# A kernel with three expert layers: when the last four ring weights of the two later layers are issued

## Chip, cores and metric

One core of a Trainium2 chip runs the whole program in one launch. The metric is device time in microseconds (us) of that core.

## What is computed

The reference is a model of three layers on 512 tokens of width 1024, in f32. The first layer has a mixer, a cross attention and a mixture of experts (32 experts of inner width 512). The two later layers have a token mixer and then a mixture of experts with 32 experts of inner width 256. Only the experts of the two later layers matter here:

```
grp_prob = softmax(xt @ w_rg + b_rg); the best group of 4, then the best 2 of its 8 experts
hid = silu(xe @ w_gate[e]) * (xe @ w_up[e]);  y = hid @ w_down[e]     # for each token of expert e
x = layernorm(alpha * x + weighted sum of the token's two y)
```

Each token goes to 2 of 32 experts, so the 1024 assignments make 32 tokens per expert on average.

## The kernel before

`moe` (line 785) is called three times: e0 for the first layer (its tiles begin with m_ or e_), e1 and e2 for the two later layers (r_, e_). It is one block with a program for each engine; order within an engine is program order, and engines meet only on semaphores.

**Routing.** VectorE (DVE) and TensorE (PE) choose experts and ranks and make a table of blocks: a block is up to 64 tokens (SLOTS) of one expert. In the two later layers all of this waits for the token mixer's result.

**Weights.** `ExpertRing` (line 735) is a ring of expert slots in SBUF. Each slot s has two parts, gate_up (part 0, 2048 KB in the later layers, loaded at L757) and down (part 1, 1024 KB, L760). The later layers have six slots, thus twelve parts in the order (0,0), (0,1), (1,0) to (5,1). The first four parts, "early", are issued during the token mixer. The other eight, "late", are issued at line 900 by SyncE (SP) at the start of `moe`, right behind the store of all token rows to DRAM (L899, 2048 KB). In e0 the ring has three slots, so six parts, of which three are early and three late. After the late loads SP waits for the table and then goes round `refill`: for expert e it waits until the expert's gate/up matmuls are done (gu_ready) and issues gate_up of expert e+6 into the slot, then waits for the expert's last output (y_ready) and issues its down part. All these loads are on one hardware DMA queue (q1).

**Tokens.** GpSimd (POOL) gathers the rows of each block from DRAM with an indirect DMA at L1246 into `landing[:, p]`, two buffers in turn, on the software queue (q0). `rows_gathered[p]` rises by 16 when such a gather has landed. The first two gathers wait for the stored rows and for `tokcol`, the token numbers made by DVE. DVE copies a landed block (L1156 for the first, L1159 for the second, L1178 for the others), PE turns it (L957, L959), DVE copies it to `xT` (L1151).

**Experts.** PE goes through the experts in order. For each it waits until gate_up has landed (line 979); each block has 32 matmul pairs for gate and up (L987, L989), a turn of the hidden rows (L967) and, once the down part has landed, eight matmuls (L1004). DVE copies the output (L1173), and POOL scatters it to DRAM (L1254). When all blocks are done, SP loads the outputs back (L924), and DVE adds and normalises.

```
def load_first(self, sp, parts):          # line 763
    for s, m in parts:
        self.load(sp, s, s, m)
...
pool.wait_ge(tokcol_ready, 1)             # line 1260
for n in range(2):
    gather(n, n)
```

Of the kernel before, what the change touches and what calls it, by code (L numbers as in the profile page):

```python
# [784 lines left out]
def moe(nc, name, k, x, rows_dram, h_rows, gain, ring, router, norm, alpha=1.0):  # L785
# [15 lines left out]
    with Stage(nc, name) as st:  # L801
# [57 lines left out]
        rows_gathered = [st.sem(f"rows_gathered{n}") for n in range(2)]  # L859
# [31 lines left out]
        def pairs_of_blocks(eng):  # L891

            return eng.value_load(pair_table[0:1, 0:1], min_val=1, max_val=MAX_BLOCKS // 2)

        with nc.Block() as block:
            @block.sync
            def _(sp):
                if h_rows is not None:
                    sp.dma_start(rows_dram.rearrange("(t p) d -> p t d", p=P), h_rows).then_inc(rows_stored, 16)  # L899
                ring.load_first(sp, ring.late)  # L900
                sp.wait_ge(table_ready, 2)

                def refill(turn_, s):

                    e = turn_ * RING + s
                    end = sp.value_load(table[0:1, 1, bass.ds(e, 1)], min_val=1, max_val=MAX_BLOCKS)
                    sp.wait_ge(gu_ready, end * 2)
                    ring.load(sp, e + RING, s, 0)
                    sp.wait_ge(y_ready, end)
                    ring.load(sp, e + RING, s, 1)  # L910

                with sp.Fori(0, TURNS - 1) as turn_:
                    for s in range(RING):
                        refill(turn_, s)
                for s in range(TAIL):
                    refill(TURNS - 1, s)

                n_pairs = pairs_of_blocks(sp)
                for n in range(2):
                    sp.wait_ge(y_stored[n], n_pairs * 16 + 32)  # L920
                for t in range(TT):
                    for j in range(2):
                        a = 2 * S * j + 2 * P * t
                        sp.dma_start(ring.back(j)[:, t, :], y_dram[a:a + 2 * P].rearrange("(p h) d -> p (h d)", p=P)  # L924
                                     ).then_inc(back_landed[j * TT + t], 16)
                    if norm.out is not None and t == 0:
                        for n in range(2):
                            sp.dma_start(norm_rows[:, n], norm.rows[n].partition_broadcast(P)).then_inc(norm_rows_landed, 16)
                if norm.out is not None:
                    for t in range(TT):  # L930
                        sp.wait_ge(finished, t + 1)
                        sp.dma_start(norm.out[t * P:(t + 1) * P], x[:, t, :]).then_inc(out_stored, 16)
                    sp.wait_ge(out_stored, 16 * TT)
# [1709 lines left out]
```

## Time and profile before

| | |
|---|---|
| time, median of 3 runs | 2899.93 us (2899.85 to 2900.85) |
| the profiled execution: its time, its span | 2899.57 us, 2896.9 us |
| PE, DVE, ACT, POOL busy | 84%, 45%, 32%, 13% |
| e1's block, from the store of rows to the last expert matmul | 1661.5 to about 1966 us |
| e2's block, the same | 2566.1 to about 2854 us |
| median time of a later gate_up load from issue to landing | 32.0 us |

"Span" is from the first to the last instruction on the core. In the windows view each row is a stretch of the span with each engine's busy time and number of instructions, the granted TensorE clock (1.00 is 2.4 GHz, 0.50 is 1.2 GHz), the mean busy share of the 16 DMA engines and the GB/s that they moved (a share can read a little over 1, since a packet counts to the stretch in which it starts). In the timeline a row is start, duration, engine, line, operation, operands, and in brackets the engine's idle time before it. "DMA to landing" is the time from an issuing instruction's start until the semaphore tells that the data has landed.

### The profile page before, as it was taken

Reading aid. Unit: us, or ns where it says so; the run is one execution under the profiler, and the core shown is the slowest. Engines: PE = TensorE matmul, PEld = TensorE weight load, DVE = VectorE, ACT = ScalarE, POOL = GpSimd, SP = SyncE. Lnnn points to the kernel's source line nnn. Section 1 sums busy time; section 2 is a strip of 40 time slices with the busy share of each in tenths; the row PEclk is TensorE's granted clock in tenths of the full one; section 3 lists DMA queues with packets and bytes.
Section 4 is the critical chain, followed back from the end, with each engine's and each line's share of the span. In section 5 each row is a group of like instructions: output and inputs, shape, how many; then the busy total and the mean of one; then the engine's idle time right before and its main releaser. Section 6 shows DMA issues by size and latency. Waiting matters only on the chain. (4 is left out here: it accounts for less than half of the span.)

```text
span 2896.9 us, 50154 instructions
## 1 busy us (share of the span) xinstructions
PE 2445.6 (84%) x18120; PEld 1919.4 (66%) x18121; DVE 1304.2 (45%) x2835; ACT 921.4 (32%) x1736; POOL 381.2 (13%) x710
## 2 busy tenths in 40 slices
PE   7987799698889868999898869995999989859783
PEld 6976698554445437776676857674777767857562
DVE  6465335421112125646553644335744844654334
ACT  3533333221111124235432323324334632223222
POOL 1000000121122110000000134430000000024332
PEclk9999899699999989999999879998999999969996
DMA  4201325599999953032122489994222222459994
GB/s 149 74 1 59 102 88 206 201 406 409 410 405 407 401 201 120 30 91 55 46 55 70 164 304 378 377 367 141 74 64 55 55 55 64 177 213 382 379 391 186
DMA packets 209397, 565.77 MB, mean 195 GB/s; under 512 B 26694, under 2 KB 170694, under 8 KB 184688
## 3 DMA queue, kind: packets, MB, share of 16 engines
q1 hardware_dynamic: 191200, 538.74, 50.0%
q0 software_dynamic: 18064, 25.23, 2.7%
q8 instruction: 86, 1.41, 0.2%
q14 instruction: 47, 0.39, 0.0%
HBM read 560.47 MB, written 36.18 MB: 206 GB/s over the span
## 5 line engine op out<-in xcount | busy, mean ns | idle before, releaser
L987 PEld LDWEIGHTS ps<-r_gate_up,e_xT 128*64 128x64 f32 x2272 | 263.8, 143 | 93.0 <-issue 89.3
L987 PE MATMUL ps<-m_gate_up,e_xT 128*64 128x256 f32 x1088 | 272.0, 414 | 62.1 <-DMA m_gate_up<-in_w_gate_up 61.3
L987 PE MATMUL ps<-r_gate_up,e_xT 128*64 128x128 f32 x2272 | 276.0, 282 | 43.9 <-DMA r_gate_up<-in_w_exp_gate_up 34.9
L1167 DVE TENSOR_TENSOR e_hid<-e_silu,ps 64x128 f32<-64x128 f32 (+1 forms) x210 | 70.2, 335 | 470.8 <-ACT e_silu L1029 467.4
L987 PEld LDWEIGHTS ps<-m_gate_up,e_xT 128*64 128x64 f32 x1088 | 160.9, 150 | 175.2 <-issue 112.1
L989 PE MATMUL ps<-r_gate_up,e_xT 128*64 128x128 f32 x2272 | 276.1, 282 | 0.0
L989 PE MATMUL ps<-m_gate_up,e_xT 128*64 128x256 f32 x1088 | 272.1, 414 | 0.0
L1029 ACT ACTIVATE e_silu<-ps 64x128 f32<-64x128 f32 (+1 forms) x210 | 63.8, 304 | 645.7 <-PE ps L989 645.7
L989 PEld LDWEIGHTS ps<-r_gate_up,e_xT 128*64 128x64 f32 x2272 | 263.7, 143 | 0.0
L2404 PE MATMUL ps<-t_hT,t0a_t0g_w 128*128 128x512 f32 x768 | 199.5, 411 | 4.6 <-DVE t0a_t0g_w L2426 2.4
L2404 PE MATMUL ps<-t_hT,t1a_t1g_w 128*128 128x512 f32 x768 | 199.1, 411 | 4.6 <-DVE t1a_t1g_w L2426 2.4
L1173 DVE TENSOR_SCALAR e_y<-ps 128x512 f32 x105 | 72.6, 691 | 249.1 <-PE ps L1004 225.4
L2404 PEld LDWEIGHTS ps<-t_hT,t0a_t0g_w 128*128 128x128 f32 x768 | 145.6, 194 | 45.9 <-issue 10.3
L2404 PEld LDWEIGHTS ps<-t_hT,t1a_t1g_w 128*128 128x128 f32 x768 | 145.3, 194 | 45.7 <-issue 10.3
L1029 ACT ACT_TABLE_LOAD x105 | 134.7, 1283 | 120.7 <-issue 119.9
L989 PEld LDWEIGHTS ps<-m_gate_up,e_xT 128*64 128x64 f32 x1088 | 160.8, 150 | 0.0
L1917 POOL TENSOR_TENSOR all_x<-all_x,t_merged 128x1024 f32<-128x1024 f32 x2 | 4.8, 2402 | 1142.0 <-PE ps L1750 1142.0
L1004 PE MATMUL ps<-r_down,e_hidT 128*64 128x512 f32 x568 | 137.5, 605 | 0.0
L1251 POOL COPY e_choicecur<-e_choicecol 128x1 uint32 x106 | 53.0, 500 | 586.0 <-DVE e_y L1173 586.0
L1246 POOL DMA_INDIRECT e_landing<-e_dram_rows,e_tokcur x115 | 116.6, 1014 | 59.4 <-issue 59.4
L1004 PE MATMUL ps<-m_down,e_hidT 128*64 128x512 f32 x544 | 124.2, 598 | 0.0
L1254 POOL DMA_INDIRECT e_dram_y<-e_y,e_choicecur x106 | 109.8, 1036 | 56.0 <-issue 55.8
(651 smaller groups left out, 4788.6 us busy)
## 6 DMA issues: line engine op xcount, KB each, us to landing
m_gate_up<-in_w_gate_up SPq DMA_DIRECT2D x32, 4096.0 KB, 38.4
r_gate_up<-in_w_exp_gate_up SPq DMA_DIRECT2D x64, 2048.0 KB, 32.0
m_down<-in_w_down SPq DMA_DIRECT2D x32, 2048.0 KB, 38.1
r_down<-in_w_exp_down SPq DMA_DIRECT2D x64, 1024.0 KB, 33.7
t0a_t0g_raw<-in_w_in SPq DMA_DIRECT2D x32, 512.0 KB, 3.8
t1a_t1g_raw<-in_w_in SPq DMA_DIRECT2D x32, 512.0 KB, 3.8
mixw_raw<-in_w_in SPq DMA_DIRECT2D x10, 1024.0 KB, 5.2
xaw_raw<-in_w_kv_x SPq DMA_DIRECT2D x8, 1024.0 KB, 5.3
```

What stands on the lines that cost most here:

```text
L987: nc.tensor.matmul(ps_gu[q][0:SLOTS], xT[:, c, :], ring.gu[s][:, 0, c, span], start=c == 0, stop=c == DC - 1)
L989: last = nc.tensor.matmul(ps_gu[q][SLOTS:P], xT[:, c, :], ring.gu[s][:, 1, c, span], start=c == 0, stop=c == DC - 1)
L1004: last = nc.tensor.matmul(ps_y[h * SLOTS:(h + 1) * SLOTS], hidT[:, f, :], ring.wd[s][:, f, h * 512:(h + 1) * 512], start=f == 0, stop=f == ...
L1029: nc.scalar.activation(silu[SLOTS:P, q], ps_gu[q][0:SLOTS], ACT.Silu).then_inc(silu_ready, 1)
L1167: vec.tensor_tensor(hid[SLOTS:P, q], silu[SLOTS:P, q], ps_gu[q][SLOTS:P], ALU.mult).then_inc(hid_ready, 1)
L1173: vec.tensor_scalar(y[:, bass.ds(g % 2, 1)].rearrange("p one d -> p (one d)"), ps_y, 1.0, None, ALU.mult).then_inc(y_copied, 1)
L1246: nc.gpsimd.indirect_dma_start(landing[:, p], None, rows_dram, bass.IndirectOffsetOnAxis(tokcur[p][:], 0), bounds_check=S - 1, oob_is_err= ...
L1251: nc.gpsimd.tensor_copy(choicecur[p][:], choicecol[:, bass.ds(n, 1)]).then_inc(choicecur_ready, 1)
L1254: nc.gpsimd.indirect_dma_start(y_dram, bass.IndirectOffsetOnAxis(choicecur[p][:], 0), y[:, p], None, bounds_check=4 * S - 1, oob_is_err=Fa ...
L1917: link(nc.gpsimd.tensor_tensor(x[:, t, :], x[:, t, :], finish[0][:, 0], ALU.mult))
L2404: last = nc.tensor.matmul(ps[:, 6, :], w[:, p, q, :], self.hT[:, r, q, :], start=q == 0 and p == r, stop=q == DC - 1 and p == LO)
```

## The change

In SP's program of `moe`, the late parts are issued in two portions. The first four late parts, (2,0) to (3,1), are issued as before. If there are more (there are in e1 and e2, not in e0), SP waits until both `rows_gathered` semaphores have reached 16, that is until the first two gathers have landed, and then issues (4,0), (4,1), (5,0), (5,1).

```
                 if h_rows is not None:
                     sp.dma_start(rows_dram.rearrange("(t p) d -> p t d", p=P), h_rows).then_inc(rows_stored, 16)
-                ring.load_first(sp, ring.late)
+                ring.load_first(sp, ring.late[:4])
+                if ring.late[4:]:
+                    for n in range(2):
+                        sp.wait_ge(rows_gathered[n], 16)
+                    ring.load_first(sp, ring.late[4:])
                 sp.wait_ge(table_ready, 2)
```

## Rows read from the trace of the kernel before

**Rows 1.** Waits of PE, 1690 to 1860 us (e1): total us, times, longest.
```profile
PE ps L957 <- DVE e_gathered L1156: 12.2, 1, 12.2
```

**Rows 2.** Waits of PE, 2690 to 2860 us (e2).
```profile
PE ps L987 <- DMA r_gate_up<-in_w_exp_gate_up: 25.4, 10, 3.7
```

**Rows 3.** Timeline of SP in e1: the first, third and fourth gate_up refill.
```profile
1707.58 0.35 SPq L757 DMA_DIRECT2D r_gate_up<-in_w_exp_gate_up  x1
...
1740.01 0.33 SPq L757 DMA_DIRECT2D r_gate_up<-in_w_exp_gate_up  x1
...
1746.49 0.33 SPq L757 DMA_DIRECT2D r_gate_up<-in_w_exp_gate_up  x1
```

**Rows 4.** Timeline of SP in e2: store of rows, part (3,1), first and fourth refill.
```profile
2566.08 0.38 SPq L899 DMA_DIRECT2D e_dram_rows<-all_x  x1
...
2570.11 1.29 SPq L760 DMA_DIRECT2D r_down<-in_w_exp_down  x1
...
2605.38 0.35 SPq L757 DMA_DIRECT2D r_gate_up<-in_w_exp_gate_up  x1
...
2624.90 0.33 SPq L757 DMA_DIRECT2D r_gate_up<-in_w_exp_gate_up  x1
```

**Rows 5.** Timeline of POOL: gathers of e0 (first), e1 (both), e2 (second).
```profile
553.02 1.14 POOL L1246 DMA_INDIRECT e_landing<-e_dram_rows,e_tokcur  x1 [0.65 <-issue]
...
1683.04 2.43 POOL L1246 DMA_INDIRECT e_landing<-e_dram_rows,e_tokcur  x1 [0.57 <-issue]
...
1686.47 0.96 POOL L1246 DMA_INDIRECT e_landing<-e_dram_rows,e_tokcur  x1 [0.54 <-issue]
...
2591.40 0.97 POOL L1246 DMA_INDIRECT e_landing<-e_dram_rows,e_tokcur  x1 [0.54 <-issue]
```

**Rows 6.** L1246 by source, e1's gathers issued at 1683.0, 1686.5, 1734.3: to landing.
```profile
DMA to landing us min/median/max: 9.2/9.2/9.2
...
DMA to landing us min/median/max: 8.1/8.1/8.1
...
DMA to landing us min/median/max: 3.0/3.0/3.0
```

**Rows 7.** The chain that ended last, in e2: start, us, what.
```profile
2587.97 8.25 DMA e_landing<-e_dram_rows,e_tokcur
```

**Rows 8.** L1246 by source, e0's first gather, then its second: issue to landing.
```profile
DMA to landing us min/median/max: 3.7/3.7/3.7
...
DMA to landing us min/median/max: 3.1/3.1/3.1
```

**Rows 9.** Windows around e0's first gathers (553) and in e1.
```profile
553.00:559.00 6.00, 1.35 (x9) 1.25 (x9) 0.69 (x1) 0.00 (x0) 5.25 (x10) 0.50 0.20 59
...
1699.00:1700.00 1.00, 1.00 (x22) 1.00 (x20) 0.29 (x1) 0.27 (x1) 0.00 (x0) 0.92 1.13 336
1702.00:1708.00 6.00, 6.00 (x84) 4.69 (x83) 2.36 (x5) 2.25 (x5) 2.19 (x5) 1.00 0.05 16
1732.00:1740.00 8.00, 8.00 (x115) 6.42 (x111) 2.88 (x6) 2.38 (x6) 4.33 (x8) 1.00 0.14 48
1740.00:1940.00 200.00, 187.64 (x2393) 144.93 (x2391) 74.49 (x142) 63.26 (x142) 88.86 (x171) 0.98 1.01 390
```

**Rows 10.** Windows in e2.
```profile
2566.00:2588.00 22.00, 5.58 (x48) 5.28 (x48) 15.76 (x74) 2.79 (x3) 0.39 (x3) 0.50 0.97 384
2604.00:2608.00 4.00, 4.00 (x45) 2.59 (x43) 0.98 (x2) 1.24 (x4) 0.00 (x0) 1.00 0.93 243
2608.00:2840.00 232.00, 204.08 (x2556) 156.77 (x2554) 79.81 (x150) 67.55 (x151) 93.28 (x180) 0.97 1.00 381
```

**Rows 11.** In e2, (3,1) at L760, then the first refill at L757: issue to landing.
```profile
DMA to landing us min/median/max: 19.9/19.9/19.9
...
DMA to landing us min/median/max: 8.8/8.8/8.8
```

**Rows 12.** The page's DMA issues, later layers' gate_up: KB each, median us to landing.
```profile
r_gate_up<-in_w_exp_gate_up SPq DMA_DIRECT2D x64, 2048.0 KB, 32.0
```

## The prediction, on record before the result

> **What bounds the kernel now.** I read the page first (PE busy 84%, DMA near its top in the expert stages), then the waits of PE in e1 and e2, then SP's and POOL's timelines at the start of both layers, and last the windows, which show what the DMA engines do.
>
> At the start of each later expert layer PE stands idle until the first gathered block has been copied: 12.2 us in e1 [rows 1]. The last part of that wait is the gather itself. It takes 9.2 us in e1 [rows 6] and 8.25 us in e2, where it lies on the chain that ended last [rows 7]. In e0, where the DMA engines are at share 0.20 [rows 9], the same instruction's gathers land after 3.7 and 3.1 us [rows 8]. So about 5 us of each first gather looks like company on the DMA engines: the eight late parts.
>
> Then the layers differ. In e1 the DMA engines run dry twice, share 0.05 at 1702 to 1708 and 0.14 at 1732 to 1740, while PE is busy all the time [rows 9]: PE sets the pace, since SP issues a refill only when PE has used a slot up. From 1740 to 1940 the share is 1.01. In e2 the engines never run dry: 0.93 at the worst spot, then 1.00 from 2608 to 2840 [rows 10], and in the later part PE waits ten times for gate_up [rows 2]. From its first load on, e2 is a queue of loads whose sum sets the end. That is the reader's main picture: the same edit comes to a stage with DMA slack and to one without.
>
> **The change, part by part.** The store of rows and the first four late parts are issued as before. Behind them SP now waits for two gathers. Queued behind the waiting instruction are the last four late parts (two of 2048 KB [rows 12], two of half that: 6.29 MB) and then every refill. PE waits for these in the end. POOL's gathers wait for nothing that stands behind SP's wait, only for the store ahead of it.
>
> *The first gather.* Rows and first four parts are 2.10 + 6.29 = 8.39 MB. In e2 the engines move 384 GB/s x 22.0 us = 8.45 MB by 2588.0 [rows 10], and part (3,1) lands at 2570.11 + 19.9 = 2590.0 [rows 4, 11]: 2 us after the bytes are counted, as the engines don't end together. The first gather's instruction takes 2.43 us in e1 and e2 [rows 5] (DVE scales x beside it; this stays), so its packets meet nearly empty engines once the last four parts are held back. In e0 the gather landed 3.7 - 1.14 = 2.56 us after its instruction ended [rows 5, 8]. With that:
> - e1: 1683.04 + 2.43 + 2.56 = 1688.0 in place of 1692.2, gain 4.2 us.
> - e2: 2587.97 + 2.43 + 2.56 = 2593.0 in place of 2596.2, gain 3.3 us.
> Bounds: none of it (the gather stays as long), and 4.6 and 3.7 us if the 3.1 us row is the measure (3.1 - 0.97 = 2.1 us after the end). I take the first row, as it is the same instruction in the same place.
>
> The Trainium skill ("DMA: Bandwidth & Descriptors", section "Queues, rings and completion order") says that each DMA engine takes turns between the queue rows that have work, a packet at a time. The gather's queue would then never wait for the weights' backlog, and holding weights back would free little; 9.2 against 3.7 us speaks for more than such sharing, but the page gives a rival, worked out below from rows.
>
> *e1.* PE starts 4.2 us earlier. It starts at 1.2 GHz, and the clock goes to 2.4 GHz just after 1699 [rows 9], some 7 us after the gather's landing; if the rise follows the earlier start a little less closely, some tenths are lost: I count 4.0. Are the held parts in time? SP goes on at 1686.47 + 3.1 = 1689.6 [rows 5, 8]; with 0.7 us until bytes flow (0.97 of 22 us in [rows 10]), 6.29 MB at 385 GB/s (16.3 us) and the 2 us of uneven ends, (5,1) lands at 1708.6. PE uses slot 4 after the fourth refill is issued, at 1746.49 - 4 = 1742 [rows 3]: over 30 us of cover. Refill one would be issued at 1703.4 and be done about 1717, refill two about 1728, and the third is issued at 1740.01 - 4.2 = 1735.8 [rows 3]: the engines still run dry before it, with some 7 us to spare. From the third refill on everything is as before, 4 us earlier. What is late next is DMA, but it moves with it. e1: -4.0 us, between -4.6 and 0.
>
> *e2.* The gain of 3.3 us at PE's start is worth nothing, since loads set the end. What counts is when the queue has moved the same bytes. Before, the first refill's gate_up landed at 2605.38 + 8.8 = 2614.2 [rows 4, 11]. After: SP goes on at 2591.40 + 3.1 = 2594.5 [rows 5, 8], bytes flow from 2595.2. Ahead of that landing are 6.29 + 2.10 MB of weights: 8.39 / 0.385 = 21.8 us, and 2 us of uneven ends: 2619.0. That is 4.8 us later; with the third and fourth gathers among them I take 5.0. Afterwards the share is 1.00 up to 2840, so nothing gives it back. Counted in idle time instead, the engines stand from 2588.0 to 2595.2, less 0.2 for two small gathers, against 0.07 x 4 = 0.3 us before [rows 10]: 6.7 us, the upper end. If the rate is 5% better with less company, 3.5 us, the lower end. The held parts are in time: (5,1) at 2595.2 + 16.3 + 2 = 2613.5, slot 4 wanted after 2624.90 - 3.3 = 2621.6 [rows 4].
>
> *e0.* Its late list has three parts; nothing changes.
>
> **Sum.** -4.0 + 5.0 = +1.0 us on the profiled execution's 2899.57 us (span 2896.9 and 2.7 around it) is 2900.6; the median is 0.36 above that execution, so 2900.9 us. From the ends, -4.6 + 3.5 = -1.1 and -3.2 + 6.7 = +3.5 us (with 0.8 us less in e1, should the clock rise later).
>
> The Trainium skill (same page, section "Rules for kernel authors") advises to issue a DMA early and wait late. e2 is where the trace agrees: 7 us without packets in a stage that has no other empty stretch. e1, with its empty stretches, is where that rule would mislead.
>
> **The rivals.**
> *Slower: gathers don't get shorter.* If the 8 to 9 us come from the gather itself in these layers (stored rows read back, the slowed 2.43 us instruction) and not from weights, e1 gains nothing, and SP is released at 2591.4 + 9.3 or so = 2600.7, 6.2 us later than above. e2 then loses 5.0 + 6.2 = 11 us: 2911 us. For it: each layer's first gather here differs from e0's. Against: e1's gather issued at 1734.3, in the stretch with share 0.14, lands after 3.0 us [rows 6, 9], and it reads the same stored rows. It decides for slower by over 0.2% once the second gather takes more than about 4 us longer than 3.1 us with little gained in e1. This is also what packet-wise turns would give.
> *Faster: the gap in e2 is made good.* If fewer bytes in flight let the later loads go faster, or PE's earlier start counts in e2 too, both layers gain: -4.0 - 3.3 = -7.3, 2892.6 us. For it: PE runs without waits until about 2700 in e2. Against: the waits after that [rows 2], and a share of 1.00 with 381 GB/s.
> *It does nothing:* the first four parts alone hold the gather up. e1 0, e2 0 to +5: within 0.2% anyhow. (3,1) landing before or at the end of the gather's instruction speaks against it.
>
> **How the numbers follow.** What a measurement of this kernel tells from no change is about 0.2%, 5.8 us. The forecast has 0.65, doing nothing 0.06, the faster rival 0.10, the slower one 0.12, and 0.07 is for sizes off beyond my ends (mostly a longer gap in e2). Within 0.2%: 0.74; faster 0.11; slower 0.15. The range reaches from some way toward the faster rival to half way to the slower: 2895.5 to 2906.5 us.
>
> **What the profile after would show.** If right: both first gathers 3.5 to 5.5 us; first refill of e1 about 4 us earlier after its row of stored tokens, and e1's whole block shorter by about 4; in e2 a window of about 7 us with share near 0.1 around 2588 to 2595, first refill issued 3 us earlier but landing 5 us later, PE's waits for gate_up up by about 8 us (5 later loads and 3 earlier start), e2's block longer by 5. Wrong, if the gathers still take over 7 us, if e2's gap is under 3 us, or if e2's end doesn't move while a gap is there.

## The result, and the profile after

| | before | changed |
|---|---|---|
| median of 20 runs each, us | 2900.39 (2894.75 to 2904.82) | 2905.68 (2898.04 to 2910.89) |
| ratio | | 1.0016, 95% interval 1.0009 to 1.0023 |
| profiled execution: time, span | 2899.57, 2896.9 | 2908.11, 2906.2 |

The change makes the kernel slower by 0.16%, some 4.6 us (2.6 to 6.7). That lies within the 0.2% that the prediction calls no change, but the interval keeps it apart from zero. The profiled execution of the changed kernel is 9.3 us longer in its span. 3.5 us of that come before e1's block begins and 2.0 us between the two blocks, where the programs are the same, so they are scatter. Both later layers are therefore measured from their own store of rows (L899).

First SP's timeline in e1 and then in e2 after the change (start, us, what). In each layer the first row is part (4,0), the first load behind SP's wait, and the second row is the first refill:

```profile
1692.82 0.33 SPq L757 DMA_DIRECT2D r_gate_up<-in_w_exp_gate_up  x1
...
1706.96 0.35 SPq L757 DMA_DIRECT2D r_gate_up<-in_w_exp_gate_up  x1
...
2597.17 0.33 SPq L757 DMA_DIRECT2D r_gate_up<-in_w_exp_gate_up  x1
...
2604.44 0.35 SPq L757 DMA_DIRECT2D r_gate_up<-in_w_exp_gate_up  x1
```

The rows of tokens are stored at 1665.0 and 2568.8 here. So SP is released 27.8 and 28.4 us after the store. The first refill is issued 42.0 and 35.6 us after it, against 46.1 [rows 3] and 39.3 [rows 4]: 4.1 and 3.7 us earlier. The next fences are the first gather of e2 on the chain that ended last, then the time to landing of e1's first gather and of e2's first refill:

```profile
2590.68 4.26 DMA e_landing<-e_dram_rows,e_tokcur
```
```profile
DMA to landing us min/median/max: 5.0/5.0/5.0
...
DMA to landing us min/median/max: 21.2/21.2/21.2
```

Both first gathers are short now: 5.0 for 9.2 us [rows 6], 4.3 for 8.25 us [rows 7]. But e2's first refill lands 35.6 + 21.2 = 56.8 us after the store, where it was 39.3 + 8.8 = 48.1 [rows 4, 11]. The windows say where the time went (columns as in [rows 10]; the last three figures are clock, DMA share, GB/s):

```profile
2568.80:2590.80 22.00, 5.58 (x48) 5.28 (x48) 15.84 (x74) 2.79 (x3) 0.48 (x3) 0.50 0.96 381
2590.80:2597.00 6.20, 1.13 (x9) 1.16 (x9) 2.89 (x2) 0.00 (x0) 5.57 (x8) 0.50 0.13 35
2597.00:2601.00 4.00, 3.22 (x31) 3.03 (x31) 1.28 (x2) 0.00 (x0) 2.75 (x7) 0.50 0.82 94
2601.00:2605.00 4.00, 4.00 (x52) 3.80 (x48) 0.58 (x2) 0.75 (x3) 0.48 (x1) 0.73 0.99 383
...
2611.00:2840.00 229.00, 196.44 (x2399) 149.88 (x2397) 75.99 (x144) 64.54 (x144) 88.79 (x171) 0.96 1.01 386
```

There is the predicted dry stretch, 6 us at share 0.13. Behind it is a stretch that was not predicted: 4 us at share 0.82 in which only 94 GB/s move. The DMA engines read as busy and carry a quarter of their usual rate. From 2611 on they are full to the end of the loads, so there is no empty stretch in which the loss could be made good.

Next come TensorE's waits after the change (total us, times, longest): e1 from 1690 to 1862 us, e1 from 1860 us on before and after, and e2 from 2690 us on. Behind them are the down matmuls by source line, e1 and e2, before and after; the figure to read there is the last start.

```profile
PE ps L961 <- DVE e_gathered L1160: 8.0, 1, 8.0
```
```profile
PE ps L987 <- DMA r_gate_up<-in_w_exp_gate_up: 9.5, 5, 2.3
PE ps L987 <- issue: 4.0, 2, 3.8
...
PE ps L991 <- DMA r_gate_up<-in_w_exp_gate_up: 15.2, 8, 4.3
PE ps L991 <- issue: 0.5, 1, 0.5
```
```profile
PE ps L991 <- DMA r_gate_up<-in_w_exp_gate_up: 22.7, 10, 3.7
PE ps L991 <- issue: 3.5, 3, 2.5
```
```profile
L1004 PE MATMUL ps<-r_down,e_hidT x304: 592/592/644, 1702.0 to 1965.4; 128*64 128x512 f32 x152
...
L1004 PE MATMUL ps<-r_down,e_hidT x264: 592/592/644, 2606.2 to 2853.2; 128*64 128x512 f32 x132
```
```profile
L1008 PE MATMUL ps<-r_down,e_hidT x304: 592/592/644, 1701.3 to 1966.2; 128*64 128x512 f32 x152
...
L1008 PE MATMUL ps<-r_down,e_hidT x264: 592/592/644, 2605.3 to 2862.6; 128*64 128x512 f32 x132
```

TensorE's wait at e1's start fell from 12.2 [rows 1] to 8.0 us. From the store, e1's last down matmul starts at 301.2 us (303.9 before), e2's at 293.8 us (287.1): -2.7 and +6.7 us. The waits for gate_up in e2's window from 2690 are no longer than before [rows 2]. In the changed kernel they begin earlier: two of them, 6.2 us, stand before 2690, where the kernel before has none. Over the whole of e2 they rise from 25.4 to 28.9 us.

### The profile page after: what moved, and what is told of

It reads as the page before. It is cut to its first block and busy times, and to the rows that moved or that the text cites. A ratio compares the mean times of both kernels' runs of the same rounds, so it can differ in the third digit from the quotient of the medians.

```text
span 2906.2 us, 50156 instructions
## 1 busy us (share of the span) xinstructions
PE 2453.6 (84%) x18120; PEld 1927.3 (66%) x18121; DVE 1302.8 (45%) x2835; ACT 920.8 (32%) x1736; POOL 381.6 (13%) x710
## 5 line engine op out<-in xcount | busy, mean ns | idle before, releaser
L2408 PEld LDWEIGHTS ps<-t_hT,t1a_t1g_w 128*128 128x128 f32 x768 | 145.4, 194 | 45.7 <-issue 10.3
L2408 PEld LDWEIGHTS ps<-t_hT,t0a_t0g_w 128*128 128x128 f32 x768 | 144.5, 193 | 45.3 <-issue 10.3
```

Source lines behind the costliest of these rows:

```text
L2408: last = nc.tensor.matmul(ps[:, 6, :], w[:, p, q, :], self.hT[:, r, q, :], start=q == 0 and p == r, stop=q == DC - 1 and p == LO)
```

## Experiments

Every kernel was timed in turns with the kernel before on one chip. The diffs are against the changed kernel, and cuts in them are marked by dots. The expectations speak of theories: in theory A held loads cost time only in a layer whose end is set by loads; theory B is the rival of each run, as it is told there.

**1. One layer at a time.**
```
+                    if name == "e1":        # e1_only; "e2" in e2_only
                         for n in range(2):
                             sp.wait_ge(rows_gathered[n], 16)
```


> The wait for the two gathers is kept in e1 and left out in e2. Theory A (a dry DMA queue costs only where DMA sets the end): e1's block about 3 us shorter as in the changed kernel (-2.8 there), e2 as before, so 3 us under the kernel before, ratio about 0.999. Theory B (the change costs the same few us wherever it stands): the e1 part slows too, +2 us or more over before. The first gather of e1 lands after about 5 us, that of e2 after about 8 us.

> The wait is kept in e2 and left out in e1. Theory A: e1 as before, e2's block about 6.6 us longer (the measured shift of the changed kernel's e2), so +6 to +7 us, ratio about 1.0023, the slowest of this set. Theory B (the loss lies elsewhere, or is spread over both): +2 us.

Measured: e1 alone 0.9987 (0.9979 to 0.9996), e2 alone 1.0027 (1.0016 to 1.0037). One part gains some 4 us, the other loses some 8; together that is the change's 1.0016 within the noise. Theory B, the same loss wherever the wait stands, falls. The next rows are TensorE's wait at e1's start in the kernel with the wait in e2 alone, and windows of e2 from 22 to 42 us after the store, first with the wait in e1 alone, then with the wait in e2 alone:

```profile
PE ps L962 <- DVE e_gathered L1161: 12.3, 1, 12.3
```
```profile
2588.36:2608.36 20.00, 10.12 (x96) 8.55 (x98) 5.55 (x7) 1.60 (x5) 8.45 (x14) 0.61 0.98 353
```
```profile
2592.17:2612.17 20.00, 14.20 (x162) 12.37 (x163) 7.12 (x10) 2.54 (x7) 10.95 (x19) 0.69 0.70 208
```

In e2, (353 - 208) GB/s x 20 us = 2.9 MB are missing at 42 us; at 385 GB/s that is 7.5 us.

**2. The wait without the gap, and the gap's length.**
```
-                    for n in range(2):
-                        sp.wait_ge(rows_gathered[n], 16)
+                    sp.wait_ge(hot_slots_ready, 1)      # no_gap: released 18 us after the store
+                    sp.wait_ge(tokcur_ready, 2)         # at_issue: 24
+                    sp.wait_ge(rows_gathered[0], 16)    # first_gather: 26 to 27
+                    sp.wait_ge(gu_ready, 2)             # late_gap: 35
```
(one of the four in each), and `six_first` with `late[:6]` and `late[6:]` in place of 4.

> In both layers the last four parts are held back, but only until the ranks are ready (the semaphore that lets TensorE make the token table), some 18 us after the store of rows, when the first four parts are still moving. Theory A: the DMA engines don't run dry, so e2 loses nothing; the last four parts are back in line before the gathers, so these take 8 to 9 us and e1 gains nothing: same as before within 1 us. Theory B (the wait on SyncE or the split of the loads costs by itself): +3 us or more, although no gap shows.

> In both layers the last four parts are held until GpSimd has copied the second block's token numbers, that is until the second gather is about to be issued, some 25 us after the store of rows and 3.3 us before the changed kernel's release. Theory A (loss in proportion to the dry time): dry stretch of 3 to 4 us in place of 6 to 7, e2 +3 to +4 us; the first gather is ahead of the weights and takes 5 to 6 us, so e1 gains 3: in all about the time before, 0 to +1 us. Theory B (most of the loss is paid for restarting an empty queue, however short it was empty): e2 +6 as before, +3 in all.

> In both layers the last four parts are held until TensorE has done the first block's gate and up, some 35 us after the store of rows, 7 us after the changed kernel's release. Theory A (e2 pays for each dry us, e1 has slack): e2 +14 us, e1 still -3 to -4, so +10 us over before, ratio 1.0035. Theory B (the loss is paid once for restarting an empty queue): the same as the changed kernel, +4 to +5 us.

> In both layers the last four parts wait for the first gather alone, released some 26 us after the store of rows, between the kernel that waits for the second gather's issue (24.5 us, e2 +4.5 us) and the changed kernel (28.4 us, e2 +7 us). Theory A (e2 pays for bytes not moved by about 42 us): e2 +5 to +6, e1 -3 to -4, +1 to +2 us in all. A side question: in the changed kernel the first weight packets after the release take 2.5 to 2.9 us each and a microsecond without any new packet follows. If that comes from an empty queue alone, it is here too; if it comes from the third gather, issued within a microsecond of the release there, the first packets here take 1.1 to 1.4 us.

> In both layers six of the late parts are issued at once and only the last two, (5,0) and (5,1), wait for the two gathers. Theory A: the queue still holds about 3 MB when the gathers are issued, so these are slowed for most of their 8 to 9 us and e1 gains 0 to 1 us; the queue is dry for at most 3 us before the release at about 33 us, so e2 loses 0 to 3 us: between -1 and +3 us in all. Theory B (any weights behind the gather do no harm, only the last four parts' start does): e1 gains 3 to 4 us here too.

Measured, with each layer's length from its store of rows to the end of its last down matmul, and e2's rate from 22 to 42 us after the store. Each length and rate is from one trace:

| kernel | ratio (95%) | e1, us | e2, us | GB/s | bytes missing against 352, as us at 385 GB/s |
|---|---|---|---|---|---|
| before | 1 | 304.5 | 287.7 | 353 | 0 |
| changed | 1.0016 (1.0009 to 1.0023) | 301.8 | 294.4 | 205 | 7.6 |
| e1_only | 0.9987 (0.9979 to 0.9996) | 302.2 | 287.2 | 353 | 0 |
| e2_only | 1.0027 (1.0016 to 1.0037) | 306.7 | 293.4 | 208 | 7.5 |
| no_gap | 1.0000 (0.9992 to 1.0009) | 306.3 | 285.4 | 352 | 0 |
| at_issue | 0.9997 (0.9987 to 1.0007) | 302.5 | 290.8 | 289 | 3.3 |
| first_gather | 1.0000 (0.9989 to 1.0012) | 303.6 | 291.2 | 280 | 3.7 |
| six_first | 1.0010 (0.9999 to 1.0020) | 305.9 | 290.6 | 293 | 3.1 |
| late_gap | 1.0018 (1.0008 to 1.0029) | 302.8 | 297.1 | 128 | 11.6 |

The wait by itself costs nothing (no_gap).

e2's loss follows the bytes that were not moved. The four kernels whose e2 misses none (with e1_at_issue below) take 285.4 to 288.0 us, 287.1 on the mean. Against that mean at_issue, first_gather, six_first, e2_only, the changed kernel and late_gap lose 3.7, 4.1, 3.5, 6.3, 7.3 and 10.0 us, for 3.3, 3.7, 3.1, 7.5, 7.6 and 11.6 us missing.

e1 gains the same whatever the gap, as long as the first gather goes ahead of the held weights. Such kernels take 301.8 to 303.6 us, 302.6 on the mean (e1_at_issue's 302.6 among them; spare_later of experiment 4, which loses its gain elsewhere, is left out). Those where it doesn't take 304.5 to 307.1, 306.1 on the mean (with the light kernels' 307.1 and 306.1). The difference is -3.5 us, and the two groups don't overlap. With six parts in front it gains nothing: any weights still in line slow the gather, not the last four alone (e2's first gather in six_first takes 8.8 us).

Theory B in its other form, a fixed price for an empty queue, would give at_issue and late_gap the same time. It falls by their ratios, whose intervals don't overlap, and by their e2, 290.8 and 297.1 us. By its ratio alone late_gap would have spoken for theory B: it costs +5 us (2 to 8), which is what B gave for this run, under my +10. Its two layers make +7 in the trace.

I had expected +14 us for e2 in late_gap, and 10 came. I had scaled up the changed kernel's own loss, which holds the slow restart of experiment 4. In late_gap the first 14 us behind the release move 1.1 MB more than in the changed kernel, worth 2.9 us at 385 GB/s; the rest of the 4 us is open.

**3. e2 with lighter loads.** In the refills of e2 only the gate half of gate_up is loaded. The up half keeps an earlier expert's weights, so e2's result is not the model's, while the work of the compute engines is the same:
```
+                    if name == "e2":
+                        sp.dma_start(ring.gu[s][:, 0]..., ring.w_gate_up[bass.ds(e + RING, 1), :, 0]...)
+                    else:
+                        ring.load(sp, e + RING, s, 0)
```


> The kernel before, but in e2 each refill brings only the gate half of gate_up (1024 KB in place of 2048 KB); the up half keeps the weights of an earlier expert, so e2's output isn't the reference's. 26 refills x 1.05 MB = 27 MB less. Both theories: e2 is no longer set by loads, and its block ends some 20 to 35 us earlier, limited by TensorE (about 38 blocks of 6.5 us and the start). It is the base for the next kernel.

> As the kernel with light refills in e2 and with the wait for the two gathers in e2 alone. Theory A (the sign is set by whether loads bound the layer): TensorE starts 3.5 to 4 us earlier and nothing takes it back, so about 3.5 us less than the light kernel without the wait. Theory B (e2's start itself is hurt by the wait, whatever the loads do later): +3 us or more over the light kernel without it.

Measured: 0.9910 (0.9895 to 0.9925) and 0.9894 (0.9877 to 0.9912), medians 2876.77 and 2871.10 us. The intervals of the two ratios overlap, but each of the four runs with the wait (2875.40 us at most) is shorter than each of the five without it (2875.43 at least). In the traces e2 takes 260.4 us without the wait and 256.4 with it, -4.0 us, and every block of e2 is 3.7 to 4.0 us earlier. The same bytes are missing as in the changed kernel (204 GB/s in the window from 22 to 42 us). TensorE's waits in e2 from 2690 us, without and with SP's wait, hold no gate_up any more:

```profile
PE ps L972 <- DVE e_hid L1172: 3.8, 18, 0.2
PE ps L992 <- issue: 0.2, 1, 0.2
```
```profile
PE ps L977 <- DVE e_hid L1177: 3.7, 18, 0.2
```
The same wait in the same layer has the other sign once loads no longer bound it.

**4. The slow restart.** In the changed kernel the first 4 us behind the release move 94 GB/s, in late_gap 246. GpSimd issues four stores of 256 bytes (L1264 before) at 26.3 to 28.5 us after e2's store of rows, just ahead of the weights. In the changed kernel their packets, 64 of 16 bytes, run until 29.2 us and the weights' first packets start at 29.3. The expectation calls it theory S that these stores hold up the weights, and theory R that the empty queue or the third gather does. The stores are moved behind the third gather, in all three layers.
```
                 for n in range(2):
                     gather(n, n)
-                for n in range(4):
-                    nc.gpsimd.dma_start(spare_dram[n:n + 1], ...)
                 ...
                 gather(2, 0)
+                for n in range(4):
+                    nc.gpsimd.dma_start(spare_dram[n:n + 1], ...)
```


> The changed kernel, with GpSimd's four small stores to the spare rows issued behind the third gather in place of between the second and the third, in all three layers. In the runs so far the first weight packets took 2.3 to 2.9 us each where SyncE was released 26.9 to 28.4 us after the store of rows, and 1.1 to 1.4 us where released at 24.5, 26.2 or 35.5; the four stores are issued at 26.3 to 28.4 us. Theory S (these stores hold up the first weight packets): now 1.1 to 1.4 us, e2's loss 5 to 6 us in place of 7, about +2 us over before. Theory R (an empty queue, or the third gather, does it): the first packets stay at 2.3 us or more, e2 +7, +3 to +5 us in all.

Measured: 1.0018 (1.0009 to 1.0027). First the 4 us behind the release in e2 in the changed kernel, late_gap and spare_later, and a restart in the kernel before, behind e1's dry stretch; then a wait of DVE in spare_later, 1700 to 1730 us.

```profile
2597.20:2601.20 4.00, 3.22 (x31) 3.15 (x32) 1.28 (x2) 0.00 (x0) 2.75 (x7) 0.50 0.82 94
```
```profile
2600.40:2604.40 4.00, 4.00 (x45) 2.77 (x47) 1.79 (x4) 1.95 (x4) 0.00 (x0) 1.00 0.77 246
```
```profile
2599.30:2603.30 4.00, 3.22 (x32) 3.08 (x32) 1.28 (x2) 0.00 (x0) 3.41 (x7) 0.50 0.75 238
```
```profile
1707.60:1711.60 4.00, 4.00 (x47) 2.77 (x47) 1.93 (x4) 1.81 (x4) 1.33 (x4) 1.00 0.94 291
```
```profile
DVE e_y L1177 <- DMA e_dram_spare<-all_ident: 3.7, 1, 3.7
```
With the stores out of the way the first sixteen weight packets took 0.7 to 2.0 us, mostly 1.0 to 1.5, where they took 2.0 to 3.5 us in the changed kernel, and 238 GB/s flow: theory S holds for the restart (one trace, both layers). The other kernels fit. Where SP is released at 26.9 to 28.4 us, beside the stores, the first packets mostly take over 2 us, in every trace and layer; where it is released at 24.2 to 26.2 or 32.5 to 35.7 us, mostly under 1.5. In first_gather the packets were slow in e1 (released at 26.9) and not in e2 (26.2). Even without the stores the restart stays below the 385 GB/s of a full stream.

The whole got no faster. The first block's output copy now waits 3.7 us for the late stores, which takes e1's gain away (305.2 us). e2 takes 293.1 us: 6.0 us over the mean of 287.1, for 6.2 us missing (232 GB/s), so it lies on the line of experiment 2, and only 1 us under the changed kernel.

**5. The gaining part alone, released earlier.** `if name == "e1": sp.wait_ge(tokcur_ready, 2)`, nothing in e2.

> e1 holds the last four parts until the second gather is about to be issued, e2 issues all at once as before. Theory A: e1 -3 to -4, e2 0, so the same gain as with the wait for both gathers in e1 alone: ratio 0.9985 to 0.999. Theory B (any held load costs): not under before.

Measured: 0.9987 (0.9976 to 0.9999), e1 302.6 us, e2 288.0 us. Like e1_only it beats the kernel before by some 4 us and the changed one by some 8.

## Why the prediction was right, and where it was off

- *The first gather gets shorter once the last four parts are held back.* Right: 5.0 and 4.3 us, where 5.0 (2.43 + 2.56) was worked out. The rival "gathers don't get shorter" is out. In the kernel before, e1's first gather does pass weights that were queued ahead of it: issued 21.5 us after the store, it lands at 30.7, while parts (4,1) to (5,1), issued at 5.6 to 6.7, land at 32.7 to 42.8. So far the trace agrees with the Trainium skill ("DMA: Bandwidth & Descriptors", section "Queues, rings and completion order"), which has each engine take turns between queues. What failed is the rival's conclusion that holding weights back would then free little: the first gathers beside full queues take 8 to 9 us and without them 4 to 5. How the turns add up to those 4 us, no run here shows.
- *e1: -4.0 us.* -2.7 in the profiled pair, -3.5 on the mean of the kernels. Right in kind, within its bounds. In the profiled pair some 4 us were there at the first block. 0.8 of them went in the fifth block, at a later gather that DVE had to wait for, and more at e1's end. There TensorE waits for loads too: from 1860 us on, 15.7 us in place of 13.5.
- *SP's release.* 27.8 and 28.4 us after the store, where 28.1 and 28.4 were worked out.
- *e2: +5.0 us.* This is the term that was mis-sized: it measured +6.7 in the profiled pair and, against the mean of experiment 2, +7.3 there and +6.3 in e2_only (+6.8 on the mean of the two), about the upper end of 6.7. The prediction let the held bytes flow at 385 GB/s from 0.7 us after the release, and had (5,1) land 47.4 us after the store and the first refill 52.9; in the trace they land at 51.1 and 56.8. Of the missing 3.7 us, the restart accounts for 2.3: 94 GB/s for 4 us costs 3.0 us, of which 0.7 were counted. The small stores of GpSimd, which I hadn't listed among the DMAs of that stretch, are the larger part of it: with them moved, (5,1) lands at 49.2. The rest is open; from 2605 to 2611 the engines move 343 GB/s. The restart at 1707.6 in the kernel before, 291 GB/s for 4 us (experiment 4), would have warned me.
- *Nothing gives e2's delay back.* Right in the main: share 1.01 to the end, and a loss that follows the missing bytes over seven kernels. The faster rival is out. A little does come back: the first refill lands 8.7 us later and e2 ends 6.7 us later. In the 230 us from 42 us after the store, 386 GB/s move in place of 383, which is worth 1.8 us; one pair of traces doesn't tell that from scatter.
- *Sum.* +1.0 forecast, +4.6 measured (2.6 to 6.7); the terms above make -3.5 + 6.8 = +3.3. The likeliest case was right in its mechanism, with signs, in both layers. Its size was not: +4.6 lies past the ends of -1.1 and +3.5 us that the sum itself gave, and 2905.68 us is only 0.8 us under the upper end of the range. That it lies in the range is in part luck: the upper end had been stretched toward the slower rival, and the restart used that room up. The lower end of e2's term has a slip: 5% off the 21.8 us leaves 3.7 to 3.9 us, not 3.5.
- *The waits for gate_up up by 8 us* in the window from 2690: they weren't, and even over the whole of e2 they rose by 3.5 us only. From its first to its last down matmul e2 takes 10.3 us more. 4.6 of them are longer busy time of TensorE, 223.9 in place of 219.3 us for as many matmuls, at a granted clock of 0.95 in place of 0.97. The prediction looked for the whole delay in waits.

## What to carry to other kernels

Holding loads back to let a small, urgent transfer through pays only where the stage's DMA engines have empty stretches later; where they are full to the end, a byte that wasn't moved is paid for at about the bandwidth. Decide it for each stage by its windows (share of DMA, and who waits late in the stage), not for each function: two calls of the same code had opposite signs here, and one of them turned when its loads were made lighter. When an empty queue is started again, look at every small DMA that is issued in those microseconds, and count its first packets at their own rate.

## What was not expected of the hardware

The first weight packets behind an empty stretch take longer than those in a stream (16 KB packets take about 0.62 us in mid-stream): mostly 1.0 to 1.5 us without the small stores, and 2.0 to 3.5 us with the four 256-byte stores just ahead. DMA share reads 0.75 to 0.82 in those first 4 us. The share alone would have called that stretch busy; only GB/s shows it.
